# Encoder layer on Trainium2: where the stores, the W-down sums and the second half's loads sit in the MLP's up projection

## The reference, cut to what matters

```python
h = h + mixed @ w_out[i]
hn = rms_norm(h, g_mlp[i])
h = h + jnp.square(jax.nn.relu(hn @ w_up[i])) @ w_down[i]      # 1024 -> 4096 -> 1024
gate = jax.nn.sigmoid(rms_norm(h, g_ple[i]) @ w_ple_gate[i])
h = h + gate * (p[i] @ w_ple_proj[i])
```

## Time and profile before

| what | value |
|---|---|
| median of 3 runs | 3340.43 us (3334.88 to 3346.74) |
| the profiled execution: its own time, its span | 3346.74 us, 3345.0 us |
| PE busy, PEld busy | 94%, 81% of the span |
| DVE, ACT, POOL busy | 56%, 43%, 43% |
| mean granted TensorE clock | 0.981 |
| Up, from its first to its last matmul | 1732.93 us to about 2469 us of the span |
| DMA, mean over the span | 148 GB/s |

### The profile page before, as it was taken

One profiled execution on the slowest core, in us unless ns is written; L12 is line 12 of the kernel. 1 busy time (PEld: TensorE's weight loads), 2 busy tenths in 40 slices (PEclk: granted clock), 3 DMA queues, 4 the chain that ended last, 5 costly groups with the idle time before them and its releaser, 6 DMA issues.

```text
span 3345.0 us, 48843 instructions
## 1 busy us (share of the span) xinstructions
PE 3159.4 (94%) x17504; PEld 2710.7 (81%) x17504; DVE 1889.6 (56%) x3199; ACT 1425.9 (43%) x2600; POOL 1437.5 (43%) x1148
## 2 busy tenths in 40 slices
PE   8999999999999999998998998788889999999998
PEld 8988888888888899996877777677778888888787
DVE  5133443888888856655566665776554444553232
ACT  4011111777777778772242222322333333434332
POOL 2133331011111156652256667666667665666222
PEclk9999999999999999998999999999999999999999
DMA  5233336103031247746734664366576568666121
GB/s 171 89 104 126 126 116 180 39 20 90 20 84 43 73 100 188 182 122 196 248 136 167 227 201 157 120 207 215 200 249 197 183 221 278 204 202 220 64 85 54
DMA packets 467406, 493.43 MB, mean 148 GB/s; under 512 B 84064, under 2 KB 377312, under 8 KB 461920
## 3 DMA queue, kind: packets, MB, share of 16 engines
q1 hardware_dynamic: 463824, 484.02, 47.0%
q10 hardware_dynamic: 3344, 6.29, 0.7%
HBM read 322.05 MB, written 168.17 MB: 147 GB/s over the span
## 4 chain that ended last, share of the span: by engine, by line
PE 73%; DVE 8%; POOL 8%; DMA 5%; issue 4%; ACT 1%; SPq 1%; POOLq 0%; DVEq 0%; ACTq 0%
PE h_acc L136 6%; PE h_acc L138 6%; PE h_acc L137 6%; PE a_acc L138 5%; PE a_acc L137 5%; PE a_acc L136 5%; PE c_pv L844 5%; PE b_pv L984 4%; DMA s_u<-e_u 3%; PE c_turned L833 3%; PE c_scores L825 3%; PE b_scores L1236 3%; PE c_scores L826 3%; DVE c_neg_half L741 3%; DVE c_a_row L774 2%
## 5 line engine op out<-in xcount | busy, mean ns | idle before, releaser
L2278 POOL TENSOR_TENSOR h_u_lo<-h_u_raw,h_u_hi 128x512 fp32r<-128x512 f32 x224 | 379.0, 1716 | 210.8 <-ACT h_u_hi L2274 210.4
L136 PE MATMUL e_acc<-e_b_hi,e_a_hi 128*128 128x512 f32 x768 | 314.0, 409 | 84.7 <-ACT e_p L2024 59.3
L741 DVE TENSOR_REDUCE c_neg_half<-c_scores 128x1 f32<-128x1024 f32 x256 | 312.8, 1222 | 83.2 <-PE c_scores L826 83.2
L136 PE MATMUL h_acc<-h_w_hi,h_u_hi 128*128 128x512 f32 x896 | 350.1, 391 | 8.0 <-DVE h_h L2372 8.0
L138 PE MATMUL h_acc<-h_w_hi,h_u_lo 128*128 128x512 f32 x896 | 349.8, 390 | 0.0
L137 PE MATMUL h_acc<-h_w_lo,h_u_hi 128*128 128x512 f32 x896 | 349.7, 390 | 0.0
L2372 DVE TENSOR_TENSOR h_h<-h_acc,h_h 128x512 f32<-128x512 f32 x224 | 153.8, 689 | 315.8 <-PE h_acc L138 303.8
L698 ACT ACTIVATE c_e<-c_scores,c_neg_max 128x1024 f32<-128x1024 f32 x256 | 286.8, 1121 | 59.2 <-DVE c_neg_max L748 51.2
L137 PE MATMUL e_acc<-e_b_lo,e_a_hi 128*128 128x512 f32 x768 | 309.8, 403 | 0.0
L138 PE MATMUL e_acc<-e_b_hi,e_a_lo 128*128 128x512 f32 x768 | 309.4, 403 | 0.0
L844 PE MATMUL c_pv<-c_v,c_at 128*128 128x128 f32 x2048 | 270.2, 276 | 0.4 <-ACT c_o L712 0.4
(11 more groups left out here) (201 smaller groups left out, 7817.2 us busy)
## 6 DMA issues: line engine op xcount, KB each, us to landing
h_u_raw<-s_u SPq DMA_DIRECT2D x224, 256.0 KB, 3.5
s_u<-e_u SPq DMA_DIRECT2D x192, 256.0 KB, 2.7
s_qkt<-a_hl SPq DMA_DIRECT2D x128, 256.0 KB, 2.8
e_a<-w_up_dram SPq DMA_DIRECT2D x64, 512.0 KB, 4.6
h_w_raw<-s_t SPq DMA_DIRECT2D x32, 1024.0 KB, 8.0
h_w_raw<-w_down_dram SPq DMA_DIRECT2D x24, 1024.0 KB, 7.8
b_kt<-s_qkt SPq DMA_DIRECT2D x64, 256.0 KB, 9.5
e_t<-w_down_dram SPq DMA_DIRECT2D x32, 512.0 KB, 6.9
```

Of the source, the lines that this page charges most:

```text
L136: nc.tensor.matmul(out, lhs_hi, rhs_hi, start=first, stop=False, skip_group_check=onto)
L741: nc.vector.tensor_reduce(neg_half[:, m, f:f + 1], bank(n, u), AX.X, ALU.max, negate=True).then_inc(S["halved"], 1)
L2278: self.nc.gpsimd.tensor_tensor(self.u_lo[q][s][:], self.u_raw[q][s][:], self.u_hi[q][s][:].bitcast(F32), ALU.subtract).then_inc(self.S["u_ ...
```

## The change

In words:

- The `t` work moves to steps 18 to 25 (`FIRST_T`), two blocks a step: the even block's subtractions on POOL, ahead of `sum_s(n, 0)`; the odd block's on DVE, at the end of its step as before. SP loads both blocks ahead of `store_1(n-1, 1)`, and stores both between `store_2(n, 1)` and `store_1(n, 0)` of the same step.
- All eight `load_xt` of the second half are issued at the end of SP's step 1; `add_t3(1)` runs in step 4.
- `store_xt(15)` stands ahead of `load_a(1)` instead of behind it.
- One counter `stored` (64 a step) takes the place of the tiles' own semaphores: every write of `u21`, `u22`, `u11`, `u12` in step n waits until all four stores of `u` tiles of step n-1 have landed, and for `s_sum` 8n.
- The sums go to a tile `s12` and a tile `s4u`, one of each instead of a pair, so `sum_s(n, j)` waits until the stores of the call before it have landed (`s_stored`). It no longer waits for the store of `u2`. The order of the seven parts in DRAM changes, and Down's `POS` with it.
- Down's first two `w` loads move from step 28 to step 26, their splits from 29 to 27.

```diff
@@ Mix, sync
             self.store_xt(sp, TILES - 2)
+            self.store_xt(sp, TILES - 1)
@@ Up.sum_s
         pool.wait_ge(S["y"], 7 * n + 6 + j)
-        pool.wait_ge(self.stored_2[j], 32 * n + 16)
-        if n:
-            pool.wait_ge(self.stored_s[j], 16 * n)
+        if 2 * n + j:
+            pool.wait_ge(S["s_stored"], 32 * (2 * n + j))
@@ Up.program
-        T_STEPS = [*range(2, 9), *range(FB + 2, FB + 11)]
+        FIRST_T = range(FB + 2, FB + 2 + FB // 2)
@@ sync
+            def store_1(n, j, u):
+                sp.wait_ge(S["s_sum"], 8 * n + 4 * j + 3)
+                sp.dma_start(pairs(n, j, 0, 2), u[:]...).then_inc(S["stored"], 16)
+                sp.dma_start(pairs(n, j, 4, 6), self.s12[:]).then_inc(S["s_stored"], 16)
                 sp.wait_ge(S["s_sum"], 8 * n + 4 * j + 4)
+                sp.dma_start(pairs(n, j, 6, 7)..., self.s4u[:]).then_inc(S["s_stored"], 16)
             for n in range(STEPS - 1):
                 self.load_a(sp, n + 1)
-                if n == 0:
-                    mix.store_xt(sp, TILES - 1)
...
+                if n in FIRST_T:
+                    m = 2 * (n - FIRST_T[0])
+                    if m:
+                        sp.wait_ge(S["t_stored"], 32 * m)
                     self.load_t(sp, m)
+                    self.load_t(sp, m + 1)
+                if n == FIRST_T[-1] + 1:
                     self.wait_t(sp)
                     down.load_w(sp, 0, 0)
                     down.load_w(sp, 0, 1)
                 if n:
+                    store_1(n - 1, 1, self.u12)
                 store_2(n, 0, self.u21, 2)
                 store_2(n, 1, self.u22, 4)
+                if n in FIRST_T:
+                    self.store_t(sp, m)
+                    self.store_t(sp, m + 1)
+                store_1(n, 0, self.u11)
+                if n == 1:
+                    for t in range(HT, TILES):
+                        mix.wait_xt(sp, t)
+                    self.wait_xt_used(sp, 0)
+                    for t in range(HT):
+                        self.load_xt(sp, 1, t)
@@ scalar (relu) and vector (y)
                 if n:
-                    dve.wait_ge(stored, times * n)
+                    dve.wait_ge(S["stored"], 64 * n)
+                    dve.wait_ge(S["s_sum"], 8 * n)
@@ vector, end of the step
+                if n in FIRST_T:
+                    self.sum_t(dve, nc.vector.tensor_tensor, 2 * (n - FIRST_T[0]) + 1)
@@ gpsimd
-                if n == 14:
+                if n == 4:
                     self.add_t3(pool, 1)
+                if n in FIRST_T:
+                    self.sum_t(pool, nc.gpsimd.tensor_tensor, 2 * (n - FIRST_T[0]))
                 self.sum_s(pool, n, 0)
```

More of the change, by code:

```diff
@@ L1727, in __init__ @@
             place(kit, f"e_u{n}", 112 + 2 * k, [P, 512]) for k, n in enumerate(("21", "22", "11", "12")))
-        self.s2 = [place(kit, f"e_s2_{j}", 66 + j, [P, 2, P]) for j in range(2)]
-        self.stored_1, self.stored_2, self.stored_s = (kit.sem_pair("e_stored_" + n) for n in ("1", "2", "s"))
+        self.s12 = place(kit, "e_s12", 66, [P, 2, 2, P])
+        self.s4u = place(kit, "e_s4u", 200.5, [P, 2, P])
         self.t = [place(kit, f"e_t{k}", 14 * k, [P, 7, 512]) for k in range(2)]
@@ L1736, in __init__ @@
             self.acc_b = ps("acc_b", 1)
-        names = "xt_in a_in prod copy a_hi a_lo a_sum b_sum b_t1 b_hi b_lo b_lop y s_sum t_stored"
+        names = "xt_in a_in stored prod copy a_hi a_lo a_sum b_sum b_t1 b_hi b_lo b_lop y s_sum s_stored t_stored"
         self.S = {name: kit.sem("e_" + name) for name in names.split()}
@@ L1920, in wait_stored @@
     def wait_stored(self, eng):
[L1921 to L1924, removed]
+        eng.wait_ge(self.S["stored"], 64 * self.STEPS)
+        eng.wait_ge(self.S["s_stored"], 64 * self.STEPS)
     def wait_t(self, eng):
@@ L1971, in _ @@
                 if n:
[L1972 to L1978, removed]
-                            mix.wait_xt(sp, t)
-                    for t in (2 * (n - 10), 2 * (n - 10) + 1):
-                        self.load_xt(sp, 1, t)
+                    store_1(n - 1, 1, self.u12)
                 store_2(n, 0, self.u21, 2)
                 store_2(n, 1, self.u22, 4)
-                store_1(n, 0, self.u11, self.u21)
+                if n in FIRST_T:
[8 more added lines that the diff above has]
+                        self.load_xt(sp, 1, t)
             n = STEPS - 1
-            store_1(n - 1, 1, self.u12, self.u22)
+            store_1(n - 1, 1, self.u12)
             self.wait_parts(sp)
@@ L2006, in _ @@
                 down.load_h(sp, 0, t)
-            store_1(n, 0, self.u11, self.u21)
+            store_1(n, 0, self.u11)
             self.wait_product(sp, 6)
             down.load_u(sp, 0, 4)
-            store_1(n, 1, self.u12, self.u22)
+            store_1(n, 1, self.u12)
             self.wait_last(sp)
@@ L2028, in relu @@
                 if n:
-                    act.wait_ge(self.stored_1[1], 16 * n)
+                    act.wait_ge(S["stored"], 64 * n)
+                    act.wait_ge(S["s_sum"], 8 * n)
                 else:
@@ L2077, in _, with y @@
         def _(dve):
-            def y(n, k, q, out, acc, part, copied, stored, times):
+            def y(n, k, q, out, acc, part, copied):
                 dve.wait_ge(S["prod"], Q * n + q + 1)
@@ L2105, in _ @@
                     self.lo_b(dve, 1, 1)
-                y(n, 1, 3, self.u21, c, self.u2, 3, self.stored_2[0], 32)
-                y(n, 3, 4, self.u22, a, self.p7, 2, self.stored_2[1], 32)
+                y(n, 1, 3, self.u21, c, self.u2, 3)
+                y(n, 3, 4, self.u22, a, self.p7, 2)
                 if n == 0:
@@ L2111, in _ @@
                 if n == 0:
-                    y(n, 5, 5, self.u11, self.acc_b[:, 0], self.p1, 1, self.stored_1[0], 16)
+                    y(n, 5, 5, self.u11, self.acc_b[:, 0], self.p1, 1)
                 if n + 1 < STEPS:
@@ L2128, in _ @@
                     self.lo_a(dve, n + 1, Q - 1)
-                if n in T_STEPS:
-                    self.sum_t(dve, nc.vector.tensor_tensor, T_STEPS.index(n))
-                if n == T_STEPS[-1] + 3:
+                if n in FIRST_T:
+                    self.sum_t(dve, nc.vector.tensor_tensor, 2 * (n - FIRST_T[0]) + 1)
+                if n == FIRST_T[-1] + 2:
                     down.lo_w(dve, 0, 0)
```

33 lines of the change are left out of this document (10 added, 23 removed).

## The result

| | median | from, to | ratio to before, 95% |
|---|---|---|---|
| before, 4 runs on the same chip | 3338.61 us | 3334.88 to 3346.74 | |
| after, 4 runs | 3453.19 us | 3452.21 to 3454.34 | 1.034 (1.032 to 1.0361) |

What follows compares the result with a forecast made beforehand. Up was taken as bound by waits, not PE; any delay of Down's start delays the end. Stage terms summed to +78.9 us on the profiled 3346.7, giving 3425.6, less 6.3 for the median: 3419 us, range 3385 to 3450.

Steps and rivals of the forecast that it cites:

- the ring: Steps 18 to 26: odd block's store waits for DVE's `sum_t`, later transfers queue behind; period 33.0 us against 20.2, +82.2 us.
- its own sign: Steps 19 to 26: prediction wrong if `y` of `u21` starts within 15 us of the step's start.
- A counter and single tiles cost nothing in a quiet step: Quiet steps: `sum_s(n-1, 1)` 1 us later, `y` of `u21` 0.5 us later; product 6 leaves 3 us, so no cost.
- Step 2 with all eight `load_xt`: Step 2 of Up: product 6 starts at 24.8 instead of 17.4, +7.3 us; step at 27 to 28 us.
- Steps 14 to 16: Up: `add_t3` gone from the chain to `add_t2`, 5.04 us plus 2.4 of restart: -7.4 us (-4 to -9).
- The start of Down: Single `s12` makes `sum_s(31, 1)` wait for `store_1(31, 0)`, issued behind four loads of `h`: +7.6 us (+5 to +9).
- Steps 0 and 1: Start of Up: `load_a(1)` behind `store_xt(15)` lands late, delaying product 2 of step 1: +5.4 us (0 to +9).
- From the profile to the median: Whole kernel: profiled execution 3346.7 becomes 3425.6 us; the median is 6.3 below, so 3419 us.
- (1): Rival, steps 19 to 26: `u12` store overtakes `t` loads, POOL's queue sets period 30 us; +58, 3398 us; chance 0.10.
- (2): Rival, steps 19 to 26: POOL's work not hidden, DVE slowed, period 36 us; +100, 3440 us; chance 0.10.
- (3): Rival: stores land in time, steps 18 to 26 take about 188 us; sum -19, 3321 us; chance 0.03.
- (4): Rival: only DMA waits, 2.5 us a block, steps 18 to 26 take 222 us; total +14, 3354 us; chance 0.05.

Runs made afterwards that it cites:

- e5: Changed kernel with each tile's own semaphores and the sums' pair of tiles and place in `u22` and `u21` restored: 3434.8 us, ratio 1.028.
- e6: Changed kernel with `t` work, `xt` loads and `add_t3` as before; counter, single tiles and place of `store_xt(15)` kept as changed: 3376.6 us, ratio 1.011.
- e7: Changed kernel with `load_a(1)` ahead of `store_xt(15)`, `load_xt` spread over steps 1 to 4, `store_1(31, 0)` ahead of the `h` loads: 3430.3 us.
- e4: Changed kernel without POOL's `sum_t`, the even blocks stored unsummed: 3453.1 us, ratio 1.033.
- e10: Changed kernel, two blocks a step kept; `store_1(n-1, 1)` ahead of `t` transfers, `t` stores an iteration later, POOL's `sum_t` and `w` loads later: 3382.5 us.
- e9: Changed kernel's order with one `t` block a step, on DVE; even blocks' sums left out, other data stored in steps 10 to 17: 3438.3 us.
- e1: Changed kernel with `store_1(n, 0)` ahead of the two `store_t` in SP's order: 3452.7 us, ratio 1.033.

## Why the prediction was right, and where it was not

Differences of the profiled executions by stage, us; what the prediction said, what came:

| stage | predicted | measured |
|---|---|---|
| before Up | 0 | -2.4 |
| steps 0 and 1 | +5.4 | +5.3 |
| steps 2 to 9 | -1.4 | +6.9 |
| steps 10 to 13 | -2.8 | +2.0 |
| steps 14 to 16 | -7.4 | -1.6 |
| steps 18 to 26 | +82.2 | +88.4 |
| steps 27 to 31 | -4.7 | -2.9 |
| Down's start, and all behind it | +7.6 | +12.3, -3.3 |
| sum | +78.9 | +104.8 |

- **What bounds the kernel, and the ring.** Right. The store of the odd block in its own iteration ties E to the stores, these to `y`, and `y` to the next E. Step 24 runs as forecast, each landmark a little later: `sum_s(n-1, 1)` at E+7.8 (6.8 predicted), the `u12` store issued at E+10.0 (9.1) and landed at E+17.8 (16.3), product 6 at E+20.4 (18.5 to 19), `sum_s(n, 0)` at E+24.0 (22.5), next E at 34.1 (33.0); over steps 19 to 26 the mean period is 33.2. Step 18 took 27.4 where 23.5 was said. Together the term is 6.2 us too small. By its own sign, `y` of `u21` later than 15 us into a step, the prediction holds: in step 24 it begins 27.1 us in.
- **A counter and single tiles cost nothing in a quiet step.** Wrong, and the one step of the prediction whose reason failed: it gave PE's product 6 as the only thing to be covered, 3 us away, and did not follow `y` of `u21` on to the end of the step. They cost about 1.0 us a step (e5 against after, steps 7 to 14), and 18.7 us over steps 2 to 31 in the old plan (e6 against before). The next fence is DVE in step 11 of the changed kernel. Its `y` begins 14.0 us into the step, held by the store issued behind `load_a`; in step 10 of the kernel before it began at 1977.07, 12.3 into the step, held by PE. Step 11 itself still takes 20.2 us, and step 12 21.7, with PE waiting 2.4 us for ACT's copy. That the later `y` pushes the sums, `sum_s4`, ACT's copy and `lo_a` into the next step is read from the order of the work and not tested by itself. Steps 10 to 13 are 85.7 where 80.9 was said, steps 27 to 31 106.5 where 104.6 was. In steps 3 to 9 the sum came out (151.0 where 150.9 was said) by luck: step 3 took 20.0 and not 22.5, which covers the 2.3 us that steps 6 to 9 are over.

```profile
2006.20 0.37 SPq L1944 DMA_DIRECT2D s_u<-e_u  x1
...
2011.72 0.69 DVE L2077 TENSOR_TENSOR e_u<-e_acc,e_u 128x512 f32<-128x512 f32 x1 [6.84 <-DMA s_u<-e_u]
```

- **Step 2 with all eight `load_xt`.** Right in kind, and the term furthest off: 35.6 us where 27 to 28 were said. The timeline of SP and the landing of the loads:

```profile
1793.87 11.46 SPq L1748 DMA_DIRECT2D e_xt<-s_xt  x8
1805.38 4.01 SPq L1755 DMA_DIRECT2D e_a<-w_up_dram  x2
1809.43 0.83 SPq L1944 DMA_DIRECT2D s_u<-e_u  x1
...
1815.66 0.69 DVE L2077 TENSOR_TENSOR e_u<-e_acc,e_u 128x512 f32<-128x512 f32 x1 [19.50 <-DMA s_u<-e_u]
...
DMA to landing us min/median/max: 4.6/7.3/8.4
```

  The issues themselves take the time: ten transfers of 512 KB in 15.5 us, and the store that DVE waits for is issued only at 1809.43, 21.6 us into the step. The prediction priced the landings at 1.5 us each and let the issues go in 0.5. e7, two loads a step, takes 6.8 us off this stage.
- **Steps 14 to 16.** The gain of `add_t3` was put at 7.4 and was 1.6. The 5.04 us of the earlier trace rows are gone from POOL, but step 14 is 23.0 us long (before 22.0), and step 15 gives only 2.6. In other runs with the same code there the stage takes 82.6 to 84.9, and with own tiles (e5) 82.5, so at most some 4 us of the 7.4 are ever seen; the 2.4 us of slower restart in the term have no row behind them, and the rest stays open.
- **The start of Down.** Right in kind, the last term mis-sized: 12.3 against 7.6 (+5 to +9). `store_1(31, 0)` behind the four loads of `h` landed 8.8 us after its last issue, as forecast, and `sum_s(31, 1)` then took 6.1 us and not the 2.8 of the earlier trace rows:

```profile
2587.77 1.93 POOL L1901 TENSOR_TENSOR e_s<-e_u,e_u 128x256 f32<-128x256 f32 x1 [16.87 <-DMA s_u<-e_s4u]
...
2590.47 2.77 POOL L1904 TENSOR_TENSOR e_u<-e_u 128x256 f32<-128x256 f32 x1
...
2593.88 6.18 POOL L2274 TENSOR_TENSOR h_u_lo<-h_u_raw,h_u_hi 128x512 fp32r<-128x512 f32 x5
...
2595.19 0.80 PE L136 MATMUL h_acc<-h_w_hi,h_u_hi 128*128 128x512 f32 x1 [19.50 <-POOL h_u_lo L2274]
```

  The sum's third operation took 2.77 us where it takes 0.72 in e7, beside this one of DVE:

```profile
2590.23 2.43 DVE L2253 TENSOR_TENSOR h_w_lo<-h_w_raw,h_w_hi 128x2048 fp32r<-128x2048 f32 x1
```

  A pair of tiles (e5) takes all of it away (48.4), the earlier store (e7) most (51.8).
- **Steps 0 and 1**: right (+5.3), and e7 gives it back by the order of one load.
- **From the profile to the median.** The sum was made against a profiled execution 8 us above the median of before (3346.7, 3338.6) and corrected by 6.3; that of after lies 1.6 below its median. Some 8 of the 34 us missed are this, the other 26 are the stages above: 8 in step 2, 6 in the ring, 5 or 6 each in steps 10 to 13, in steps 14 to 16 and at Down's start, 2 in steps 27 to 31, less some 6 before Up and behind Down's start. The mechanism and the order of the terms held; nearly every size was too small.
- **The rivals.** (1) fell: the `u12` store landed 7.8 us after its issue, behind the loads. (2) fell by e4; that its time, 3440, lies nearer to the measured one than the forecast does is luck. Both totals are 3 us too high for their own stage costs (+58 gives 3395, +100 gives 3437). (3) fell as said, the stores do not make it. (4) would have been right for the stage if the order had been kept: e10 has 217.6 where the rival said 222.

## What to carry to other kernels

A transfer's place in a shared issue queue is a dependency as real as a semaphore: before a store is moved into the iteration that makes its data, list everything queued behind it and ask whether any of that is needed for the data itself; if so, the loop has become a ring whose length is the sum and not the maximum of its parts. Test an order and an amount of work apart, as e9 and e10 do, since a slow stage that looks overloaded may have an idle queue. And put a small store that someone waits for ahead of the large loads, even in a kernel that seems tuned: that took 1% off this one.

## What the runs showed of the hardware that was not expected

- One DVE operation on 128x512 f32 tiles takes 0.69 us with POOL idle and 1.23 with POOL at work on SBUF tiles (e1), and POOL's 128x512 operation 1.26 us or up to 1.74 beside DVE. At the start of Down two of POOL's 128x256 operations took 1.93 and 2.77 us, where e7's take 0.72; each ran into a 128x2048 subtraction of DVE (2.3 and 2.4 us long) and ended 0.6 us after it, as if it had stood until that was done. An earlier start of one engine can therefore lengthen the other's chain by as much as it wins.
- An issue can itself become slow. Of the eight `load_xt` in one go the first took 0.53 us to issue, the second 1.30 and the last up to 1.80, 11.46 us in all; two of the same loads in one step of e7 took 1.26 us together. It is not the number of 512 KB transfers alone: the four loads of `t` in step 24, issued right behind two of `a`, took 0.43 to 0.50 us each. The cause stays open.
